# Forgetting-attention denominators in four 32-column groups, summed at the end of a query tile

## The chip, the cores and the metric

The kernel runs on the 8 cores of one Trainium2 chip. Each core works on one sequence of the batch and needs no other core. The metric is the device time of the slowest core in microseconds. Below, PE is TensorE, ACT is ScalarE, DVE is VectorE and POOL is GpSimd.

## The reference

One decoder layer on x of shape 8 x 2048 x 2048 (batch, sequence, model width). A combined projection feeds two groups of 8 heads each, with head size 128. What the change touches is the first group, forgetting attention (called FoX in the kernel):

```
s = q @ k.T * scale + cum[query] - cum[key]     # cum: running sum of log f
s = where(key <= query, s, -inf)
p = softmax(s)                                  # exp(s) / sum over the keys
o = p @ v
```

The kernel takes exp(s) without the division, sums it over the keys (the denominator), and multiplies the finished o by one over that sum. The second group is sliding-window attention with sinks. The output projection, norms, and a squared-ReLU MLP with d_ff 8192 follow.

## The kernel before

Everything is laid out with features on the partitions and tokens along the free dimension. The order of all work is written by one Python program. Each engine gets its own instructions in the order in which the program emits them, and waits are put in where one engine needs what another made. So an instruction that waits holds up all that were emitted behind it on its engine.

FoX runs head by head (8 heads), in `fox` (L1079), over query tiles j = 0 to 3 of 512 tokens, and inside a tile over 4j+4 key blocks kb of 128 keys. That is 40 steps in a head, 320 in all. In the last four blocks of a tile only the columns from c0 = 0, 128, 256, 384 on are computed, since the rest is masked. A step is made of three parts:

- `qk` (L1028): PE multiplies the key block by the query tile into one of three score banks (SF); in the last four blocks it adds the mask.
- `expo` (L1049): DVE subtracts the forget bias, in place in the bank; ACT writes exp of it as bf16 into one of NPB = 6 buffers Pb.
- `pv` (L1058): PE adds v times Pb into the output bank (OB[0], bank 4), and a 128x128 matrix of ones times Pb into the denominator bank (DB, bank 6). So every one of the 128 partitions of that bank holds the full sum over keys.

The loop at L1110 emits for step i: `qk` of step i+3 (LA = 3, L1075), filler, `pv` of step i, `expo` of step i+3, filler. A score bank is taken again three steps later, so `qk` of i+6 needs the exp of i+3 to be done.

The filler is other PE work that is fed in between (`Fill`, L700): projections of later heads in groups of 16 matmuls of 512 columns, evacuated by ACT or DVE from two banks, and the columns of the modulation (`mod_slot`, L485). `fw` (L1100) says how much is fed in. In heads 0 and 1 it is some 11 matmuls a step; in heads 2 to 6 it is 128 / 41.5, that is 3.08 a step, given half before `pv` and half after the step's `expo`. They come in bursts of four. In head 7 the filler is the first output tile, fed from its seventh step on.

`mod_slot` already uses the groups of 32 columns. Four matmuls with weights of 128x32 (`condpad`) write partitions 0-31, 32-63, 64-95 and 96-127 of one bank, each with its own moving operand of 512 columns. `fg_mm` (L768) does the same.

At the end of a query tile, `pv` emits the normalisation: ACT takes Ln of the denominators into `rr`, DVE copies the output bank to SBUF (`acc`), ACT takes Exp of -`rr`, DVE multiplies the two into `mix`. The next tile's first `pv` writes the same two banks, so it waits for the Ln and for the copy.

Of the kernel before, what the change touches and what calls it, by code (L numbers as in the profile page):

```python
# [7 lines left out]
BF16 = mybir.dt.bfloat16  # L8
AF = mybir.ActivationFunctionType
ALU = mybir.AluOpType  # L10
# [5 lines left out]
TS = 512  # L16
# [325 lines left out]
def program(nc, stack, orders, dry, T):  # L342
# [7 lines left out]
    B = T["bufs"]  # L350


    mix, mixF, hT = B["mix"], B["mixF"], B["hT"]
# [10 lines left out]
    rstd = [B["rstd0"], B["rstd1"]]  # L364
    rr, stage = B["rr"], B["stage"]
    qrot = B["qrot"]
    cosT, sinT = B["cosT"], B["sinT"]
    ident, maskc, mswa = B["ident"], B["maskc"], B["mswa"]
    Ctok, condpad, wfg = B["Ctok"], B["condpad"], B["wfg"]
# [3 lines left out]
    lf, Cf = B["lf"], B["Cf"]  # L373
    ones, modT, bmod, gv, Av = B["ones"], B["modT"], B["bmod"], B["gv"], B["Av"]
    onesF = B["onesF"]
    sqb = [B["sq0"], B["sq1"]]
    accs = [B["acc0"], B["acc1"]]
    WO = [B[f"WO{i}"] for i in range(16)]
# [10 lines left out]
    def mm(out, lhsT, rhs, start, stop):  # L389
        return (out.ap, lhsT.ap, rhs.ap, start, stop)  # L390

    def pe(mms, r, w, extra=()):
        def fn(e):
            ins = None
            for (o, l, rh, st, sp) in mms:
                ins = e.matmul(o, lhsT=l, rhs=rh, start=st, stop=sp)  # L396
            return ins
        return P.op("pe", fn, r, w, extra=extra)

    def act(out, in_, func, bias=None, scale=1.0):  # L400
        r = [in_]
        kw = {}
        if isinstance(bias, Acc):
            r.append(bias)
            kw["bias"] = bias.ap
        elif bias is not None:
            kw["bias"] = bias
        if isinstance(scale, Acc):
            r.append(scale)
            kw["scale"] = scale.ap  # L410
        else:
            kw["scale"] = scale
        return P.op("act", lambda e: e.activation(out=out.ap, in_=in_.ap, func=func, **kw), r, [out])  # L413

    def tt(out, a, b, op, eng="dve"):
        return P.op(eng, lambda e: e.tensor_tensor(out=out.ap, in0=a.ap, in1=b.ap, op=op), [a, b], [out])  # L416
# [12 lines left out]
    def cp(out, a):  # L429
        return P.op("dve", lambda e: e.tensor_copy(out=out.ap, in_=a.ap), [a], [out])  # L430
# [40 lines left out]
    class St:  # L471
        sb = 0
        pb = 0
        ob = 0
# [290 lines left out]
    F = Fill()  # L765
# [259 lines left out]
    def fox_list(h):  # L1025
        return [(h, j, kb) for j in range(NT) for kb in range(4 * j + 4)]

    def qk(st):  # L1028
        h, j, kb = st
        if kb == 0:  # L1030
            n = 4 * h + j
            for m in range(n, n + len(cfs)):
                if m // 4 < 8 and (m < 8 or h >= 2) and (m // 4, m % 4) not in cf_slot:
                    cf_load(m // 4, m % 4)
        bk = banks[SF[St.sb % 3]]
        St.sb += 1
        c0 = max(0, kb - 4 * j) * 128
        diag = kb >= 4 * j
        q = qT[h % 2](slice(j * TS + c0, j * TS + TS))
        kk = kT[h % 2](slice(kb * 128, kb * 128 + 128))  # L1040
        mms = [mm(bk(c0, TS), kk, q, True, not diag)]
        r = [kk, q]
        if diag:
            mms.append(mm(bk(c0, c0 + 128), ident(), maskc(), False, True))
            r += [ident(), maskc()]
        pe(mms, r, [bk()])
        steps[st] = (bk, c0)

    def expo(st):  # L1049
        h, j, kb = st  # L1050
        bk, c0 = steps[st]
        tt(bk(c0, TS), bk(c0, TS), cf_slot[(h, j)](slice(c0, TS)), ALU.subtract)
        p = Pb[St.pb % NPB]
        St.pb += 1
        act(p(slice(c0, TS)), bk(c0, TS), AF.Exp, bias=Ctok(slice(kb * 8 + h, kb * 8 + h + 1)))
        steps[st] = (p, c0)

    def pv(st):  # L1058
        h, j, kb = st
        p, c0 = steps.pop(st)  # L1060
        nkb = 4 * j + 4
        ob = banks[OB[0]]
        db = banks[DB]
        v = V_OF[h](kb, slice((h % 2) * 128, (h % 2) * 128 + 128))
        pp = p(slice(c0, TS))
        pe([mm(ob(c0, TS), v, pp, kb == 0, kb == nkb - 1), mm(db(c0, TS), ones(), pp, kb == 0, kb == nkb - 1)],
           [v, pp, ones()], [ob(), db()])
        if kb == nkb - 1:
            os = accs[1]
            act(rr(), db(), AF.Ln)  # L1070
            cp(os(), ob())
            act(rr(), rr(), AF.Exp, scale=-1.0)
            tt(mix(h, slice(j * TS, j * TS + TS)), os(), rr(), ALU.mult)

    LA = 3  # L1075

# [2 lines left out]
    def fox(segs, after=None):  # L1079

        L = [st for sg in segs for st in fox_list(sg[0])]
        n = len(L)
        seg = {sg[0]: sg for sg in segs}

        def begin(i):
            h, j, kb = L[i]
            if h in done:
                while done[h] < j:
                    F._one()
            qk(L[i])  # L1090

        jobs = {sg[0]: sg[1]() for sg in segs if sg[0] < 7}
        hs = [sg[0] for sg in segs]

        def push(h):
            F.main += jobs[h] if h in jobs else seg[h][1]()
            nx = hs[hs.index(h) + 1:]
            F.upnext = jobs[nx[0]][0] if nx and nx[0] in jobs else after

        def fw(i):  # L1100
            h = L[i][0]
            pos = i % 40
            return seg[h][2] / (40 - seg[h][3] + LA / 2) / 2 if pos >= seg[h][3] else 0

        push(hs[0])
        for i in range(LA):
            begin(i)
            F.fill(fw(i))
            expo(L[i])
        for i in range(n):  # L1110
            if i and i % 40 == 0:
                push(L[i][0])
            if i + LA < n:
                begin(i + LA)
            F.fill(fw(i))
            pv(L[i])
            if i + LA < n:
                expo(L[i + LA])
            F.fill(fw(i))


    SPB = Pb
# [87 lines left out]
    def qk_(h):  # L1210
# [7 lines left out]
        def gen():  # L1218
# [9 lines left out]
    j3 = qk_(3)  # L1228
    j6 = vpair(I_V + 6, vX)
    fox([(0, lambda: [sk_(0), svpair(), sq_(0), sq_(1), sq_(2), sq_(3)], 64 * 5 + 128, 0),  # L1230
         (1, lambda: [sk_(1), sq_(4), sq_(5), sq_(6), sq_(7), qk_(2)], 64 * 7, 0)], j3)
    F.drain()
# [107 lines left out]
    def last_head():  # L1340
# [8 lines left out]
    cfs.append(qrot)  # L1349
    St.cf = 0  # L1350
    fox([(2, lambda: [vpair(I_V + 4, vZ)], 128, 0)]
        + [(h, lambda h=h: [qk_(h + 1)], 128, 0) for h in range(3, 7)]
        + [(7, last_head, 4 * 34, 6)])
# [198 lines left out]
def build():  # L1552
# [33 lines left out]
    B = {}  # L1586

    def buf(name, off, dims, dt):
        B[name] = Buf(nc, name, off, dims, dt)
        return off + B[name].nbytes  # L1590
# [12 lines left out]
    o = RS  # L1603
    for i in range(5):
        o = buf(f"ring{i}", o, [2048], BF16)
    for nm in ("qT0", "kT0"):
        o = buf(nm, o, [S], BF16)
    buf("Cf", o, [S], F32)
    o = buf("vts", o, [16, 256], BF16)
    buf("lf", o, [S], F32)  # L1610
    buf("vZ", o, [16, 256], BF16)
    o = buf("skT", o, [2, S], BF16)
    for i in range(2):
        buf(f"rstd{i}", o, [TS], F32)
        o = buf(f"cfb{i}", o, [TS], F32)
# [4 lines left out]
    for nm in ("qT1", "kT1"):  # L1620
        o = buf(nm, o, [S], BF16)
    o = buf("vX", o, [16, 256], BF16)
# [3 lines left out]
    for i in range(NPB):  # L1626
        o = buf(f"Pb{i}", o, [TS], BF16)
    o = buf("stage", o, [TS], F32)
    o = buf("rr", o, [TS], F32)
    buf("wfg", o, [KC * 32], BF16)  # L1630
    o = buf("qrot", o, [TS], F32)
    o = buf("ident", o, [128], BF16)
    o = buf("maskc", o, [128], BF16)
    o = buf("mswa", o, [256], BF16)
    o = buf("Ctok", o, [128], F32)
    o = buf("condpad", o, [KC, 32], BF16)
# [7 lines left out]
    o = RS  # L1644
    for i in range(2):
        o = buf(f"Y{i}", o, [16, TS], F32)
    for i in range(NRB):
        o = buf(f"rung{i}", o, [2048], BF16)
# [7 lines left out]
    o = max(o, end1)  # L1656
    o = buf("ones", o, [128], BF16)
    o = buf("onesF", o, [128], F32)
    o = buf("bvb", o, [8], BF16)
    o += 112  # L1660
    o = buf("wob", o, [16], F32)
    o += 64
    o = buf("modT", o, [96], F32)
    o = buf("bmod", o, [96], F32)
    o = buf("gv", o, [4, KC], F32)
    o = buf("Av", o, [4, KC], F32)
    for i in range(2):
        buf(f"qh{i}", o + 4096 * i, [2048], BF16)
    for i in range(2):
        o = buf(f"sq{i}", o, [TS], F32)  # L1670
    for i in range(4):
        buf(f"sqs{i}", o - 4096 + 1024 * i, [256], F32)
    for i in range(2):
        o = buf(f"acc{i}", o, [TS], F32)
    assert BASE + o <= nc.sbuf_usable_end, (BASE + o, nc.sbuf_usable_end)
    T["bufs"] = B
    with ExitStack() as stack:
        T["banks"] = [Bank(stack.enter_context(nc.psum_tensor(f"bank{i}", [128, 512], F32)), i) for i in range(8)]
        orders = program(nc, stack, {}, True, T)
        program(nc, stack, orders, False, T)  # L1680
# [50 lines left out]
```

How the kernel before makes its waits and increments, by code:

```python
                def body(e, mine=mine):  # L259
                    have = {}
                    for o, ws in mine:
                        need = {}
                        for d in ws:
                            s, v = d.sig
                            need[s] = max(need.get(s, 0), v)
                        for s, v in need.items():
                            if have.get(s, 0) < v:
                                e.wait_ge(sems[s], v)
                                have[s] = v
                        if o.fn is not None:
                            ins = o.fn(e)
                            if o.sig is not None:
                                ins.then_inc(sems[o.sig[0]], 16 if o.dsem is not None else 1)
```

## Time and profile before

| what | value |
|---|---|
| median of 3 runs (range) | 2980.88 us (2980.04 to 3171.43) |
| the profiled execution | 2982.57 us, span of its slowest core (core 5) 2981.0 us |
| spans of the 8 cores | 2970.1 to 2981.0 us, granted clock 0.992 to 0.997 |
| PE busy | 2865.3 us, 96% of the span |
| DVE busy | 942.0 us, 32% |
| ACT busy | 776.5 us, 26% |
| POOL busy | 449.2 us, 15% |
| FoX, heads 0 and 1 | some 236 to 500 us from the span's start |
| sliding-window heads | some 500 to 617 us |
| FoX, heads 2 to 7 | some 617 to 978 us |

The profile is of the slowest core. Matmuls are pipelined: a row's duration reaches into the next matmul, so what a matmul costs is read as the distance from its start to the next start. An idle time in brackets on a row is what stood between the modelled end of the one before and this start, and names what ended it.

### The profile page before, as it was taken

To read this page: it belongs to the slowest core of one execution; us is meant where nothing else is said; L and a number is where in the kernel's file an instruction comes from. 1 tells how busy PE (TensorE), PEld (TensorE's weight loads), DVE (VectorE), ACT (ScalarE), POOL (GpSimd) and SP (SyncE) were. 2 spreads that over 40 slices of the span, in tenths; PEclk is the share of its full clock that TensorE was granted. 3 is DMA by queue.
4 is the path that set the end of the run, shared out by engine and by line. 5 is a ranking of instruction groups with operands and counts; after the bars stand their busy time and mean duration, and the time that the engine had idled before them with its cause. 6 is when DMAs were issued, how large, how long until landed. Compare 5 with 4: busy or idle time off the path is not lost.

```text
span 2981.0 us, 39533 instructions; the slowest of 8 cores (2970.1 to 2981.0 us)
## 1 busy us (share of the span) xinstructions
PE 2865.3 (96%) x15292; PEld 1393.3 (47%) x15292; DVE 942.0 (32%) x1510; ACT 776.5 (26%) x1276; POOL 449.2 (15%) x597
## 2 busy tenths in 40 slices
PE   3899999999998999999999999999999999999997
PEld 1466444664444444444444444444444444444446
DVE  1434664455554476431111000000333101111015
ACT  2213454655554355331111000000211000111112
POOL 1010000000001565300000111111000000000222
PEclk9999999999999999999999999999999999999999
DMA  9966665335544334644444555555788544445844
GB/s 218 213 117 119 104 106 93 64 65 92 89 82 92 99 129 169 127 78 77 75 75 78 92 98 95 91 99 109 160 188 190 95 74 75 78 78 109 155 76 149
DMA packets 107032, 325.96 MB, mean 109 GB/s; under 512 B 11584, under 2 KB 28224, under 8 KB 100448
## 3 DMA queue, kind: packets, MB, share of 16 engines
q0 software_dynamic: 58320, 211.97, 44.2%
q1 hardware_dynamic: 48528, 111.46, 11.5%
q8 instruction: 124, 2.03, 0.3%
q14 instruction: 60, 0.49, 0.1%
HBM read 493.32 MB, written 42.01 MB: 180 GB/s over the span
## 4 chain that ended last, share of the span: by engine, by line
PE 86%; DVE 3%; DMA 3%; ACT 3%; issue 2%; POOL 2%; DVEq 0%; ACTq 0%; POOLq 0%; SPq 0%
PE bank L396 86%; DMA rmod<-wMA 3%; POOL acc L416 2%; DVE bank L416 1%; ACT rr L413 1%; ACT Pb L413 1%; ACT sq L413 1%; DMA cfb<-crow 0%; ACT qrot L413 0%; DVE sq L421 0%; DVE bank L421 0%; DVE Y L416 0%; ACT acc L413 0%; DVE y L416 0%; DMA rung<-wD 0%
## 5 line engine op out<-in xcount | busy, mean ns | idle before, releaser
L396 PE MATMUL bank<-mix,rung 128*128 128x512 bf16 x4096 | 885.0, 379 | 0.0
L396 PE MATMUL bank<-a,rung 128*128 128x512 bf16 (+1 forms) x4096 | 858.4, 372 | 1.7 <-DMA rung<-wD 1.7
L396 PEld LDWEIGHTS bank<-mix,rung 128*128 128x128 bf16 x4096 | 400.8, 98 | 484.3 <-issue 1.7
L396 PEld LDWEIGHTS bank<-a,rung 128*128 128x128 bf16 x4096 | 400.7, 98 | 458.4 <-issue 1.9
L396 PE MATMUL bank<-hT,ring 128*128 128x512 bf16 x1536 | 397.0, 382 | 1.7 <-DVE sq L421 1.3
L413 ACT ACTIVATE a<-bank 128x512 bf16<-128x512 f32 x256 | 152.8, 597 | 914.4 <-DVE bank L427 913.5
L427 DVE TENSOR_SCALAR bank<-bank 128x512 f32<-128x512 f32 x256 | 166.1, 695 | 647.1 <-PE bank L396 647.1
L413 ACT ACTIVATE Pb<-bank,Ctok 128x512 bf16<-128x512 f32 (+1 forms) x320 | 193.0, 623 | 268.2 <-DVE bank L416 265.6
L396 PE MATMUL bank<-mix,WO 128*128 128x512 bf16 x1024 | 234.1, 382 | 13.5 <-ACT sq L413 12.2
L416 POOL TENSOR_TENSOR acc<-acc,sq 128x512 f32<-128x512 f32 x172 | 215.8, 1267 | 187.5 <-ACT sq L413 182.5
L396 PEld LDWEIGHTS bank<-hT,ring 128*128 128x128 bf16 x1536 | 146.4, 98 | 155.8 <-issue 10.3
L207 POOL DMA_DIRECT2D rung<-wU x128 | 68.1, 532 | 743.9 <-PE bank L396 710.0
L207 POOL DMA_DIRECT2D rung<-wD x124 | 66.2, 534 | 717.5 <-PE bank L396 689.2
L396 PE MATMUL bank<-ring,hT 128*128 128x256 bf16 x1280 | 169.5, 278 | 3.5 <-DVE bvb L430 2.6
L416 DVE TENSOR_TENSOR bank<-bank,cfb 128x512 f32<-128x512 f32 x240 | 142.3, 614 | 80.2 <-PE bank L396 74.3
L396 PEld LDWEIGHTS bank<-mix,WO 128*128 128x128 bf16 x1024 | 98.2, 98 | 136.3 <-issue 27.3
L430 DVE COPY mixF<-bank 128x512 f32<-128x512 f32 x32 | 20.6, 686 | 421.4 <-PE bank L396 421.4
L396 PEld LDWEIGHTS bank<-ring,hT 128*128 128x128 bf16 x1280 | 125.5, 100 | 47.4 <-issue 13.7
L396 PE MATMUL bank<-Pb,ones 128*128 128x512 bf16 (+3 forms) x444 | 130.8, 328 | 0.0
L413 ACT ACTIVATE sq<-bank 128x512 f32<-128x512 f32 x30 | 17.9, 597 | 396.5 <-DVE mixF L430 396.5
L396 PE MATMUL bank<-qT,kT 128*128 128x512 bf16 (+1 forms) x320 | 112.3, 352 | 9.1 <-ACT Pb L413 8.7
L207 POOL DMA_DIRECT2D ring<-wMB x64 | 33.8, 528 | 349.5 <-PE bank L396 337.8
(145 smaller groups left out, 1765.7 us busy)
## 6 DMA issues: line engine op xcount, KB each, us to landing
rung<-wU POOLq DMA_DIRECT2D x128, 512.0 KB, 6.3
rung<-wD POOLq DMA_DIRECT2D x124, 512.0 KB, 6.3
ring<-wMB POOLq DMA_DIRECT2D x64, 512.0 KB, 6.7
ring<-wA POOLq DMA_DIRECT2D x34, 512.0 KB, 6.4
Y<-xP SPq DMA_DIRECT2D x16, 1024.0 KB, 6.1
x1s<-Y SPq DMA_DIRECT2D x16, 1024.0 KB, 3.9
xstA<-xP SPq DMA_DIRECT2D x8, 1024.0 KB, 15.9
rmod<-wMA POOLq DMA_DIRECT2D x16, 512.0 KB, 21.8
```

Of the source, the lines that this page charges most:

```text
L207: return self.op(eng, lambda e: e.dma_start(out=oa, in_=ia), [in_], [out], dsem=dsem, extra=extra)
L396: ins = e.matmul(o, lhsT=l, rhs=rh, start=st, stop=sp)
L413: return P.op("act", lambda e: e.activation(out=out.ap, in_=in_.ap, func=func, **kw), r, [out])
L416: return P.op(eng, lambda e: e.tensor_tensor(out=out.ap, in0=a.ap, in1=b.ap, op=op), [a, b], [out])
L427: return P.op(eng, lambda e: e.tensor_scalar(out=out.ap, in0=a.ap, scalar1=sc, scalar2=None, op0=op), r, [out])
L430: return P.op("dve", lambda e: e.tensor_copy(out=out.ap, in_=a.ap), [a], [out])
```

## The change

The matmul of ones moves out of the step. Steps only collect their Pb buffer in `held`. At every fourth key block (kb % 4 == 3) the four collected blocks are summed together. In the query tiles j = 1 to 3 that is one group of four matmuls with weights of ones 128x32, each into its own 32 partitions of the denominator bank; the groups of a tile add up there. So each set of 32 partitions holds the sum over every fourth block. In tile j = 0 the four matmuls keep the full 128x128 ones.

At the end of a tile with j > 0, `den_split` writes the bank in two bf16 parts into `rrh`: ACT copies it (the high part), and DVE subtracts that copy from the bank (the low part). It is emitted behind the `expo` of that step. Two steps later, `den_fin` multiplies both parts by the 128x128 ones into the denominator bank. That adds up the 128 partitions, so the sum is 32 times too large, which the Ln's scale of 1/32 takes out. The Ln, the Exp and the multiplication into `mix` come after it, two steps later than before, in all tiles. The copy of the output bank stays where it was. `rrh` lies in the same bytes as `rr`. At the end of a call of `fox`, 12 units of filler are fed before the last `den_fin`.

```diff
+    rrh = B["rrh"]
+    ones32 = ones().re(ones.h[:, 0:32])
...
+    held = []
+    later = []
+
     def pv(st):
         h, j, kb = st
         p, c0 = steps.pop(st)
...
-        pe([mm(ob(c0, TS), v, pp, kb == 0, kb == nkb - 1), mm(db(c0, TS), ones(), pp, kb == 0, kb == nkb - 1)],
-           [v, pp, ones()], [ob(), db()])
+        pe([mm(ob(c0, TS), v, pp, kb == 0, kb == nkb - 1)], [v, pp], [ob()])
+        held.append((p, c0))
+        if kb % 4 == 3:
+            mms = []
+            for c, (pc, cc0) in enumerate(held):
+                if j:
+                    mms.append(mm(db(cc0, TS, p=(32 * c, 32 * c + 32)), ones32, pc(slice(cc0, TS)), kb == 3, kb == nkb - 1))
+                else:
+                    mms.append(mm(db(cc0, TS), ones(), pc(slice(cc0, TS)), c == 0, c == 3))
+            pe(mms, [pc(slice(cc0, TS)) for pc, cc0 in held] + [ones()], [db()])
+            del held[:]
         if kb == nkb - 1:
             os = accs[1]
-            act(rr(), db(), AF.Ln)
             cp(os(), ob())
-            act(rr(), rr(), AF.Exp, scale=-1.0)
-            tt(mix(h, slice(j * TS, j * TS + TS)), os(), rr(), ALU.mult)
+            return (h, j, db)
+        return None
+
+    def den_split(e):
+        h, j, db = e
+        if j:
+            act(rrh(0), db(), AF.Copy)
+            tt(rrh(1), db(), rrh(0), ALU.subtract)
+
+    def den_fin(e):
+        h, j, db = e
+        if j:
+            pe([mm(db(), ones(), rrh(i), i == 0, i == 1) for i in range(2)], [ones(), rrh()], [db()])
+        act(rr(), db(), AF.Ln, scale=1.0 / 32 if j else 1.0)
+        act(rr(), rr(), AF.Exp, scale=-1.0)
+        tt(mix(h, slice(j * TS, j * TS + TS)), accs[1](), rr(), ALU.mult)
...
             F.fill(fw(i))
-            pv(L[i])
+            e = pv(L[i])
             if i + LA < n:
                 expo(L[i + LA])
+            if e:
+                den_split(e)
+                later.append((i + 2, e))
             F.fill(fw(i))
+            if later and later[0][0] == i:
+                den_fin(later.pop(0)[1])
+        F.fill(12)
+        for _, e in later:
+            den_fin(e)
+        del later[:]
...
     o = buf("stage", o, [TS], F32)
+    buf("rrh", o, [2, TS], BF16)
     o = buf("rr", o, [TS], F32)
```

## Rows read from the trace of the kernel before

**Rows 1.** The page, the chain of work that ended last, by engine and by line.

```profile
PE 86%; DVE 3%; DMA 3%; ACT 3%; issue 2%; POOL 2%; DVEq 0%; ACTq 0%; POOLq 0%; SPq 0%
PE bank L396 86%; DMA rmod<-wMA 3%; POOL acc L416 2%; DVE bank L416 1%; ACT rr L413 1%; ACT Pb L413 1%; ACT sq L413 1%; DMA cfb<-crow 0%; ACT qrot L413 0%; DVE sq L421 0%; DVE bank L421 0%; DVE Y L416 0%; ACT acc L413 0%; DVE y L416 0%; DMA rung<-wD 0%
```

**Rows 2.** Stretches: us, then busy us (count) of PE, PEld, DVE, ACT, POOL.

```profile
236.00:500.00 264.00, 258.43 (x1606) 129.24 (x1604) 147.29 (x240) 111.99 (x197) 25.28 (x48) 1.00 0.60 101
...
617.00:978.00 361.00, 333.67 (x1985) 168.53 (x1983) 196.66 (x342) 186.24 (x313) 30.17 (x49) 0.98 0.49 87
```

**Rows 3.** Groups of instructions on TensorE; busy us, mean ns, idle before.

```profile
L396 PE MATMUL bank<-mix,rung 128*128 128x512 bf16 x4096 | 885.0, 379 | 0.0
...
L396 PE MATMUL bank<-ring,condpad 128*32 128x512 bf16 x256 | 25.6, 389 | 1.3 <-DVE modT L416 1.3
```

**Rows 4.** Order of time on TensorE; columns start us, us, instruction, count.

```profile
242.94 1.03 PE L396 MATMUL bank<-hT,ring 128*128 128x512 bf16 x4
243.90 0.40 PE L396 MATMUL bank<-ring,condpad 128*32 128x512 bf16 x4
244.23 1.04 PE L396 MATMUL bank<-hT,ring 128*128 128x512 bf16 x4
```

**Rows 5.** Order of time, all engines, around the end of a query tile (head 6).

```profile
863.61 0.38 PE L396 MATMUL bank<-qT,kT 128*128 128x512 bf16 x1
...
863.93 0.27 PE L396 MATMUL bank<-Pb,ones 128*128 128x256 bf16 x1
...
864.04 1.03 PE L396 MATMUL bank<-hT,ring 128*128 128x512 bf16 x4
864.09 0.70 DVE L416 TENSOR_TENSOR bank<-bank,cfb 128x512 f32<-128x512 f32 x1 [0.70 <-PE bank L396]
...
864.88 0.69 ACT L413 ACTIVATE Pb<-bank,Ctok 128x512 bf16<-128x512 f32 x1 [0.72 <-DVE bank L416]
...
865.12 0.22 PE L396 MATMUL bank<-Pb,vX 128*128 128x128 bf16 x1
...
865.45 1.03 PE L396 MATMUL bank<-hT,ring 128*128 128x512 bf16 x4
865.49 0.60 ACT L413 ACTIVATE rr<-bank 128x512 f32<-128x512 f32 x1
865.50 0.69 DVE L430 COPY acc<-bank 128x512 f32<-128x512 f32 x1 [0.71 <-PE bank L396]
866.18 0.63 ACT L413 ACTIVATE rr<-rr 128x512 f32<-128x512 f32 x1
...
866.45 0.38 PE L396 MATMUL bank<-Pb,vX 128*128 128x512 bf16 x1
...
866.91 0.69 DVE L416 TENSOR_TENSOR mix<-acc,rr 128x512 bf16<-128x512 f32 x1 [0.72 <-ACT rr L413]
...
867.52 1.89 DVE L416 TENSOR_TENSOR bank<-bank,cfb 128x512 f32<-128x512 f32 x3
...
868.31 1.88 ACT L413 ACTIVATE Pb<-bank,Ctok 128x512 bf16<-128x512 f32 x3 [1.50 <-DVE bank L416]
...
869.14 0.38 PE L396 MATMUL bank<-qT,kT 128*128 128x512 bf16 x1 [0.59 <-ACT Pb L413]
...
872.80 0.38 PE L396 MATMUL bank<-qT,kT 128*128 128x512 bf16 x1
```

**Rows 6.** The same view, TensorE, a tile end with more beside it (head 5).

```profile
824.76 0.22 PE L396 MATMUL bank<-Pb,vZ 128*128 128x128 bf16 x1
...
834.74 0.38 PE L396 MATMUL bank<-qT,kT 128*128 128x512 bf16 x1
```

**Rows 7.** Who waited for whom, 617 to 980 us; total us, times, longest.

```profile
PE bank L396 <- ACT Pb L413: 8.7, 15, 1.6
...
PE bank L396 <- ACT rr L413: 4.2, 6, 1.2
PE bank L396 <- DVE acc L430: 3.0, 4, 0.9
```

## Prediction

> **What bounds the kernel now.** I read the chain of waits first: 86% of it is TensorE's matmuls [rows 1]. So time is won by giving PE less to do, or lost by making it wait. Next, the busy times of the two stretches with FoX [rows 2]. In heads 0 and 1 PE is busy 258.4 of 264 us for 80 steps, 3.3 us a step. In heads 2 to 7 it is busy 333.7 of 361 us for 240 steps, 1.5 us a step; DVE and ACT are busy only 54% and 52% there, yet PE has gaps. Then the waits [rows 7]: PE waited 8.7 us for an exp (it had to free a score bank), 4.2 us for ACT's `rr` and 3.0 us for the copy of the output bank, all at tile ends. Last, one tile end in order of time [rows 5], to see which chain makes these gaps.
>
> A gap is wider than its bracket, since the bracket starts at a matmul's modelled end. A full matmul costs 885.0 / 4096 = 0.216 us from start to start [rows 3], while its row lasts 0.38.
>
> **What leaves PE.** The cost of a ones matmul goes with its columns: 256 columns took 0.11 us (863.93 to 864.04) [rows 5]. Each of the 24 tiles with j > 0 has four masked-end blocks of 512, 384, 256 and 128 columns, together 2.5 full ones: 24 x 2.5 x 0.216 = 13.0 us. Before these stand 4, 8 or 12 full blocks, 24 in a head, 192 in all: 41.5 us. Together 54.5 us go. The eight j = 0 tiles keep theirs.
>
> **What comes to PE.** 48 full groups and 24 masked-end ones, 72 groups of four. The kernel before has this very operation in its modulation columns. The burst at 242.94 should hand over after 4 x 0.216 at 243.80; the four start at 243.90, and the next matmul at 244.23 [rows 4]. So the group costs 0.43 us, twice one matmul and half of four. 48 such places in the trace lie between 0.42 and 0.44, this one stands for them. The whole of the 256 gives the same order: 25.6 us of busy time for 64 groups is 0.40 [rows 3]. 72 x 0.43 = 31.0 us. The bounds are 0.22 (one matmul) and 0.86 (four in a row); I take 0.43, the same shape measured. In a masked-end group the longest member still has 512 columns, so I take no less there. The final sums add 24 x 2 x 0.216 = 10.4 us. PE's work: -54.5 + 31.0 + 10.4 = **-13.1 us**.
>
> The Trainium skill has a rule that prices the group otherwise (TensorE: Matmul & The Clock Gate, Measured speedup vs the span model): a packed group spans one matmul plus about 4 ns for each further tile. By it, a group would be an estimated 0.23 us and PE's work 14 us less again. The same skill's TensorEngine Tiling (Array Packing), Key Properties, says that changing the tiling mode drains the array; the 0.1 us that stands ahead of the group at 243.90 agrees with the second page, so the sum goes by the row.
>
> **What the moved end of a tile costs.** Two things come to the in-order queues: ACT's copy and DVE's subtraction (24 each, some 0.6 and 0.7 us by the nearest rows, the Ln and the copy of the output bank). In busy time both engines have room. What counts is the order. Call the start of the tile's last `pv` zero (865.12) and take the links from [rows 5]: `pv` to copy of the output bank 0.38; DVE to its next instruction 0.61 (866.91 to 867.52); DVE to the ACT instruction that needs it 0.79 (867.52 to 868.31); ACT to its next 0.60 (three in 1.88, the last taking 0.69); ACT to ACT that needs it 0.69 (Ln to Exp); ACT to DVE 0.73 (866.18 to 866.91); ACT to a PE that waits 0.83 (868.31 to 869.14); DVE to a waiting PE 0.95 (865.50 to 866.45).
>
> Before: Ln 0.37, Exp 1.06, product 1.79, bias of step i+3 at 2.40, exp 3.19, PE's `qk` of i+6 at 4.02. All read straight off the rows. PE's work up to there is 0.11 + 2 x 0.216 + 4 x 0.216 + two bursts of filler 1.73 = 3.13, so 0.89 us is lost, of which the row's bracket shows 0.59 and the rest is the copy's wait at 866.45 and the modelled tail.
>
> After: copy of the output bank 0.38, bias of i+3 at 0.99, exp 1.78, ACT's copy 2.38, subtraction 3.11, bias of i+4 at 3.72 and of i+5 at 4.33, exp of i+5 5.12. The final sum on PE can start at 3.11 + 0.95 = 4.06. PE gets there after `pv` and group 0.49, two `qk` and two `pv` 0.86, and 2.5 steps of filler 1.66, at 3.0: it stops for a microsecond, and behind it stands all its work, since PE is in order. The Ln stands on ACT behind the exp of i+5: 5.72, Exp 6.41, product 7.14, and behind it on DVE the bias of i+6 at 7.75, exp 8.54, and `qk` of i+9 on PE at **9.37**. PE's work from zero to there is 0.49 + ten `qk` and `pv` 2.16 + final sum 0.43 + the next group 0.43 + 5.5 steps of filler 3.65, or four bursts 3.45 as in these rows: 6.96. So 2.4 us are lost, in two places (final sum, `qk` of i+9) and a little at the next group, which waits for the Ln at 5.72 + 0.83.
>
> Before, the same stretch runs from 865.12 to 872.80, 7.68 us. So a clean end grows by 1.7, of which 0.16 is more work inside it (0.43 x 3 against 1.13 us of ones); the lost time grows by 1.5. Four of the ten j = 1 and 2 ends in heads 2 to 6 take 7.68 or 7.69. The longest takes 9.98 (824.76 to 834.74) [rows 6]: evacuations of filler stand in its queues, and PE has a modulation group besides. I add the same lateness to the chain but the room grows too, and there I take no growth. Over all I take 0.9 us, between 0 and 1.5, weighted by four clean ends in ten. 17 ends in heads 2 to 7 have j > 0 and a next tile; those that lead into a new head have shorter blocks in chain and work alike. 17 x 0.9 = **+15.3 us**.
>
> **What costs nothing.** The six such ends in heads 0 and 1: PE has 5.5 steps x 3.3 = 18 us of work over a chain of 9.4; without that filler they would cost the same 1.5. The j = 0 ends: no split, and the Ln moves behind the exp of i+5, so the chain ends at about 7.6 against some 6.9 of work, a loss as large as now. `expo` of i+3 must wait at every group for the release of its Pb buffer, but its bias and link (0.48 from `qk`, 863.61 to 864.09, and 0.79) take as long as PE needs from that `qk` through filler, `pv` and group (1.3 us); it is due three steps later. The last end is covered by 12 matmuls of filler (2.6 us). No DMA is added or moved.
>
> Sum: -13.1 + 15.3 = +2.2 us on the profiled execution's 2982.57, which lies 1.7 above the median of the runs. That gives 2984.8 for such an execution, 2983 as a median; I say **2984**.
>
> **The rivals.**
>
> *Slower: the wait for ACT's copy on DVE.* Behind the blocked subtraction also lie filler evacuations, and one ahead of the chain adds its 0.6 to 0.7. If every end pays 1.5 + 0.6, it is 17 x 2.1 = 35.7 - 13.1 = +22.6: 3005. For it speaks that each engine is in order and every link above is measured. Against it: the ends with evacuations already have longer PE work. It decides from 13.1 / 17 = 0.8 us an end; above that the kernel gets slower. Chance 0.24.
>
> *Faster: the ends get no worse.* The old chain to `qk` of i+6 is gone (it would be ready at 1.78 + 0.83 = 2.6), and if PE has enough beside the new one, only the -13.1 is left, or with half of today's loss (17 x 0.9 / 2) -21: 2962 to 2970. Against it stand 9.37 us of chain over 7 us of work. Chance 0.21.
>
> *The groups do not run side by side.* Then 72 x 0.86 + 10.4 - 54.5 = +17.8, and with the ends 3016. Weights of ones from one tile, four Pb buffers as moving operands: nothing in that differs from [rows 4]. Chance 0.03.
>
> *The groups cost one matmul.* If the 0.2 us around the modulation groups belongs to their own weights or neighbours, a group costs 0.22 to 0.23, PE's work falls 14 us more, and what of it lies inside the chains is lost again, about half: 2970 to 2977. This is what the span model of the Trainium skill's clock gate page would bring. 48 places without an exception speak against it. Chance 0.05.
>
> **How the numbers follow.** The forecast has 0.47, its own range 2975 to 2993. The range that leaves out two in ten reaches from the faster rival to the slower one, 2960 to 3006. What a measurement can tell from no change is 2%, 60 us; no case reaches that far. Slower by more needs groups in a row and ends of 3 us together, 0.02; faster by more has no mechanism, 0.01; within 2%: 0.97.
>
> **What would show it.** Groups of four `ones` of 128x32, 0.43 from start to start; a PE wait for DVE's `rrh` of about 0.9 us, 17 times in heads 2 to 7; DVE waiting for ACT's `rrh`, 0.7 or more each; PE's wait for an exp coming 9 us after a tile's end, not 4; heads 0 and 1 shorter by some 3 us (a quarter of 13.1), heads 2 to 7 longer by some 5. Wrong it would be if heads 2 to 7 got shorter, or if heads 0 and 1 did not.

## Result and the profile after

The changed kernel took 2999.82 us (median of 5 runs, 2995.56 to 3293.65) against 2980.88 us (5 runs): ratio 1.0064, 95% interval [1.0051, 1.0077]. It is slower by 19 us, inside the predicted range of 2960 to 3006, 16 us above the predicted 2984.

Times of single executions below are those of the profiled ones, and ratios leave out executions in which cores ran at a lowered clock throughout.

Rows that name no core are those of a kernel's slowest core: 5 in the kernel before, 4 in the changed one, 3 in e6.

First the page of the changed kernel: span, busy time of PE, DVE and ACT, and the chain by engine.

```profile
span 2998.0 us, 39742 instructions; the slowest of 8 cores (2990.3 to 2998.0 us)
...
PE 2859.8 (95%) x15340; PEld 1376.1 (46%) x15340; DVE 952.1 (32%) x1534; ACT 787.3 (26%) x1300; POOL 450.2 (15%) x597
...
PE 85%; DVE 4%; ACT 3%; DMA 3%; issue 3%; POOL 2%; DVEq 0%; ACTq 0%; POOLq 0%
```

PE's busy time fell from 2865.3 to 2859.8 us while the span grew by 17 (of two profiled executions; the 19 us are of medians): PE has less to do and waits more. Its new instructions in heads 2 to 7, in groups as in [rows 3]:

```profile
L398 PE MATMUL bank<-Pb,ones 128*32 128x512 bf16 x162 | 21.8, 400 | 2.4 <-ACT rr L415 2.4
...
L398 PE MATMUL bank<-rrh,ones 128*128 128x512 bf16 x36 | 10.7, 377 | 7.2 <-DVE rrh L418 7.0
```

And who waited for whom there (total us, times, longest), the answer to [rows 7]:

```profile
ACT Pb L415 <- PE bank L398: 29.8, 22, 3.7
...
PE bank L398 <- ACT sq L415: 14.2, 6, 4.7
PE bank L398 <- ACT Pb L415: 11.2, 15, 1.1
...
PE bank L398 <- DVE rrh L418: 7.0, 12, 1.0
PE bank L398 <- DVE acc L432: 6.6, 9, 1.8
...
PE bank L398 <- ACT acc L415: 4.4, 1, 4.4
```

PE's waits for an exp are 11.2 us (8.7 before), there are 7.0 us of waits for the split's low part, 6.6 for the copy of the output bank (3.0), and, in head 7 and just behind it, 14.2 and 4.4 for the output tile's squares and first sum (7.7 and 1.3 before, shown further below). The first row is the release of held buffers: ACT waited 29.8 us for PE, but ACT is not the bound.

Where the 19 us are, from PE's first `qk` of head 0, of head 2 and of head 7, its last `pv`, and its first matmul of the MLP:

| stage, us | before, core 1 | before, core 5 | after, core 1 | after, core 5 |
|---|---|---|---|---|
| heads 0, 1 and the sliding-window heads | 389.8 | 390.2 | 387.4 | 385.2 |
| heads 2 to 6 | 280.5 | 282.1 | 289.0 | 288.6 |
| head 7 | 72.3 | 77.1 | 84.6 | 84.5 |
| to the MLP | 210.8 | 210.8 | 214.5 | 214.5 |

So packing pays where filler is plentiful (2 to 5 us), heads 2 to 6 lose 6 to 9, head 7 loses 7 to 12, and the stage behind it 4. Past that point, cores 1 and 5 take as long as before to about 1 us.

The clean tile end of the changed kernel in order of time (head 6, the tile of [rows 5]):

```profile
863.37 0.22 PE L398 MATMUL bank<-Pb,vX 128*128 128x128 bf16 x1
...
863.52 0.39 PE L398 MATMUL bank<-Pb,ones 128*32 128x512 bf16 x4
863.70 0.69 DVE L432 COPY acc<-bank 128x512 f32<-128x512 f32 x1 [0.54 <-PE bank L398]
...
863.85 0.39 PE L398 MATMUL bank<-qT,kT 128*128 128x512 bf16 x1
...
865.09 0.69 ACT L415 ACTIVATE Pb<-bank,Ctok 128x512 bf16<-128x512 f32 x1 [1.15 <-PE bank L398]
...
865.68 0.59 ACT L415 ACTIVATE rrh<-bank 128x512 bf16<-128x512 f32 x1
866.37 0.69 DVE L418 TENSOR_TENSOR rrh<-bank,rrh 128x512 bf16<-128x512 f32 x1 [1.37 <-ACT rrh L415]
866.98 1.29 DVE L418 TENSOR_TENSOR bank<-bank,cfb 128x512 f32<-128x512 f32 x2
...
867.21 0.59 PE L398 MATMUL bank<-rrh,ones 128*128 128x512 bf16 x2 [0.60 <-DVE rrh L418]
...
867.76 1.28 ACT L415 ACTIVATE Pb<-bank,Ctok 128x512 bf16<-128x512 f32 x2 [1.50 <-DVE bank L418]
...
868.94 0.59 ACT L415 ACTIVATE rr<-bank 128x512 f32<-128x512 f32 x1
...
869.62 0.63 ACT L415 ACTIVATE rr<-rr 128x512 f32<-128x512 f32 x1
...
869.68 0.40 PE L398 MATMUL bank<-Pb,ones 128*32 128x512 bf16 x4 [0.15 <-ACT rr L415]
...
870.36 0.69 DVE L418 TENSOR_TENSOR mix<-acc,rr 128x512 bf16<-128x512 f32 x1 [1.51 <-ACT rr L415]
...
870.97 1.89 DVE L418 TENSOR_TENSOR bank<-bank,cfb 128x512 f32<-128x512 f32 x3
...
871.75 1.88 ACT L415 ACTIVATE Pb<-bank,Ctok 128x512 bf16<-128x512 f32 x3 [1.50 <-DVE bank L418]
...
872.58 0.38 PE L398 MATMUL bank<-qT,kT 128*128 128x512 bf16 x1 [1.11 <-ACT Pb L415]
```

Every link of the predicted chain that these rows show is there. From the last `pv` at 863.37: ACT's copy 2.31 later (predicted 2.38), subtraction 3.00 (3.11), final sum 3.84 with a wait of 0.60 (4.06), Ln 5.57 (5.72), product 6.99 (7.14), bias of i+6 7.60 (7.75), and `qk` of i+9 at 9.21 after a wait of 1.11 (9.37). The group costs 0.43 beside FoX's own work: `pv` of 128 columns at 863.37 takes 0.06, and the next `qk` starts at 863.85. The wait for the split's low part was forecast as some 0.9 us, 17 times; it came 12 times, 7.0 us together.

### The profile page after: what moved, and what is told of

Same layout as the page of the kernel before. It is cut to its first block, busy times and chain, and to the rows that moved or that the text cites. A ratio compares the mean times of both kernels' runs of the same rounds, so it can differ in the third digit from the quotient of the medians.

```text
span 2998.0 us, 39742 instructions; the slowest of 8 cores (2990.3 to 2998.0 us)
## 1 busy us (share of the span) xinstructions
PE 2859.8 (95%) x15340; PEld 1376.1 (46%) x15340; DVE 952.1 (32%) x1534; ACT 787.3 (26%) x1300; POOL 450.2 (15%) x597
## 4 chain that ended last, share of the span: by engine, by line
PE 85%; DVE 4%; ACT 3%; DMA 3%; issue 3%; POOL 2%; DVEq 0%; ACTq 0%; POOLq 0%
PE bank L398 85%; DMA rmod<-wMA 3%; POOL acc L418 2%; DVE bank L418 1%; ACT Pb L415 1%; ACT rr L415 1%; ACT sq L415 1%; DVE acc L432 0%; DVE bank L423 0%; ACT qrot L415 0%; DVE Y L418 0%; DVE sq L423 0%; ACT rrh L415 0%; DMA rung<-wD 0%; ACT acc L415 0%
## 5 line engine op out<-in xcount | busy, mean ns | idle before, releaser
L398 PE MATMUL bank<-qT,kT 128*128 128x512 bf16 (+1 forms) x320 | 113.0, 354 | 11.7 <-ACT Pb L415 11.2
L432 DVE COPY y<-bank 128x512 f32<-128x512 f32 x32 | 20.6, 686 | 191.7 <-PE bank L398 191.7
```

## The experiments

Each was a full kernel on all 8 cores. Stages as above, heads 2 to 6 / head 7 / to the MLP, on one core with all matmul records (core 1, but 2 for e1 and 5 for e4); before is 280.5 / 72.3 / 210.8 and the change 289.0 / 84.6 / 214.5. The cores of one execution differ, in heads 2 to 6 and in the last stage by up to 3 us and in head 7 by up to 5. Differences in the text are between profiled executions (before 2982.57). The ratios carry the spread of all executions that they take in, so the intervals are wide beside the differences here.

| kernel | profiled execution, us | ratio to before [95%] | stages, us |
|---|---|---|---|
| the change | 2999.82 | 1.0064 [1.0051, 1.0077] | 289.0 / 84.6 / 214.5 |
| e1 packed, old end | 2969.00 | 0.9943 [0.9912, 0.9975] | 274.1 / 74.0 / 211.1 |
| e2 held, full ones, late end | 3000.26 | 1.0021 [0.9979, 1.0064] | 276.7 / 83.5 / 211.2 |
| e3 packed, late end, no final sum | 2964.75 | 0.9936 [0.9913, 0.9959] | 269.2 / 82.2 / 211.1 |
| e4 split early | 2989.84 | 1.0012 [0.9986, 1.0037] | 276.9 / 83.5 / 217.1 |
| e5 product late | 2974.01 | 0.9972 [0.9949, 0.9995] | 272.6 / 78.7 / 217.0 |
| e6 both | 2962.55 | 0.9915 [0.9879, 0.9950] | 263.6 / 78.4 / 216.0 |
| e7 both, head 7 alone | 2994.57 | 1.0034 [1.0002, 1.0067] | 288.6 / 79.2 / 215.7 |
| e8 both, and the last product later | 2958.26 | 0.9949 [0.9918, 0.9981] | 263.2 / 77.5 / 212.6 |
| e9 as e8, output tile 0 evacuated at once | 2942.09 | 0.9875 [0.9854, 0.9896] | 263.1 / 65.0 / 210.5 |
| e10 before, evacuated at once | 2967.43 | 0.9977 [0.9941, 1.0013] | 280.5 / 64.3 / 210.0 |
| e11 the change, evacuated at once | 2979.16 | 0.9994 [0.9952, 1.0036] | 290.1 / 68.6 / 211.0 |

**e1, packing alone.**

```diff
             os = accs[1]
+            act(rr(), db(), AF.Ln, bias=1.0)
             cp(os(), ob())
-            return (h, j, db)
+            act(rr(), rr(), AF.Exp, scale=-1.0)
+            tt(mix(h, slice(j * TS, j * TS + TS)), os(), rr(), ALU.mult)
```

> Groups of four as in the change, but the tile's end as before: Ln, Exp and product at the last pv, straight from the bank. The final sum over the groups is left out (each 32 partitions keep the sum of every fourth block, and the Ln takes a bias of 1). My theory (the packing saves PE what the rows say, the deferred end costs it): 54.5 - 31.0 = 23.5 us less PE work, and the tile ends lose 0.3 us more than before at 17 places, since the group stands ahead of the Ln: -18 us, ratio 0.994. Rival A (a group costs more than 0.43 us beside FoX's own work, up to four matmuls in a row): +7 to +12 us, ratio 1.002 to 1.004, and groups 0.86 apart in the trace. Rival B (holding the Pb buffers makes the exp wait): ratio near 1.00 with PE waiting for exps inside the tiles.

It came out at 2969.00, 13.6 us below before, where -18 was expected. Packing saves, and Rival A is out. Heads 2 to 6 gain 6.4 us, and in them PE's waits for exps grew from 6.1 to 17.8 us: the end's chain starts behind the group, and a shorter PE meets the same chain. All 17 of these waits stand at `qk` of step i+6 behind a tile's end and none inside a tile, so Rival B is out too.

**e2, holding and the late end alone.**

```diff
-                if j:
-                    mms.append(mm(db(cc0, TS, p=(32 * c, 32 * c + 32)), ones32, ...
-                else:
-                    mms.append(mm(db(cc0, TS), ones(), pc(slice(cc0, TS)), c == 0, c == 3))
+                mms.append(mm(db(cc0, TS), ones(), pc(slice(cc0, TS)), kb == 3 and c == 0, kb == nkb - 1 and c == 3))
...
     def den_split(e):
         h, j, db = e
-        if j:
-            act(rrh(0), db(), AF.Copy)
-            tt(rrh(1), db(), rrh(0), ALU.subtract)
+        return
...
     def den_fin(e):
         h, j, db = e
-        if j:
-            pe([mm(db(), ones(), rrh(i), i == 0, i == 1) for i in range(2)], ...
-        act(rr(), db(), AF.Ln, scale=1.0 / 32 if j else 1.0)
+        act(rr(), db(), AF.Ln, scale=1.0)
```

> Blocks held in fours and the end of the tile two steps late as in the change, but with 128x128 ones in all tiles, so no packing, no split, no final sum. PE's work is that of before. My theory: the chain without copy and subtraction ends at 7.55 us after the last pv against 7.3 us of PE work, so 0.3 us is lost at an end where 0.9 was: -10 us in heads 2 to 7, ratio 0.997. Rival B (holding the buffers, or the late Ln by itself, is what costs): as slow as the change, ratio 1.005 or more.

Half a miss. Heads 2 to 6 gain 3.8 us (10 were expected with head 7), so holding is not what costs. But head 7 went from 72.3 to 83.5: the late end, without copy, subtraction or final sum, makes nearly all of the change's loss there. Holding is in e2 as well, but also in e1, where head 7 takes 74.0 to 76.1. The ratio's interval holds 1, so the sum of both decides nothing; the stages do. (Its profiled execution reached FoX some 20 us late on two cores, so its 3000 says little.)

**e3, the change without split and final sum** (`den_split` returns at once, `den_fin` has no matmuls, the Ln takes bias=1.0 and scale=1.0).

> The change without ACT's copy, DVE's subtraction and PE's final sum (left out: the sum over the groups, and the Ln takes a bias of 1); Ln, Exp and product stay two steps late. My theory: 23.5 us less PE work, 0.7 us lost at an end instead of 0.9: -27 us against before, ratio 0.991, and against the change -46, of which 10.4 is the final sum's own work and the rest the chain. Rival A (dear groups): -27 + 31 = +4 us, ratio 1.001. Rival C (the late product alone makes the wait, the split has no part in it): ratio 1.003, since only the final sum's 10.4 us goes.

35 us below the change; -46 was expected. The sum over the groups is left out, as in e1. Heads 2 to 6 carry 20 of them, of which 30 final matmuls x 0.216 = 6.5 are work and 13 waiting: Rival C, by which only the final sum's own work would go, is out. Head 7 stays at 82.2 (79.3 to 83.1 on the cores), which is the larger part of what is missing. In e2 and e3, late end but no final sum, the stage behind head 7 takes 211.1 to 211.3 us: the 3.7 us that the change loses there come with the split and the final sum.

**e4, copy and subtraction ahead of the bias subtraction.**

```diff
             e = pv(L[i])
-            if i + LA < n:
-                expo(L[i + LA])
             if e:
                 den_split(e)
                 later.append((i + 2, e))
+            if i + LA < n:
+                expo(L[i + LA])
```

> The change with copy and subtraction emitted ahead of the expo of that step, not behind it. My theory: subtraction at 1.33 us after the last pv instead of 3.11, so the final sum can start at 2.3 while PE gets there at 3.0, no wait for rrh in the trace; exp of i+5 at 3.95, product 5.97, qk of i+9 at 8.2 instead of 9.2 to 9.4; an end loses 1.1 us instead of 2.4: 17 x 1.3 = 22 us less than the change, 2978, ratio to before 0.999. Rival C (only the late product counts): qk of i+9 waits as long as in the change, 2990 or more, ratio 1.003.

No wait for `rrh` is left, and the clean end takes 8.18 us (8.2 expected). Heads 2 to 6 are 12 us shorter than in the change; in all it is 10 us by the profiled executions, 12 by the medians, and not 22: head 7 and the stage behind it keep their losses.

**e5, the product one step later.**

```diff
         act(rr(), rr(), AF.Exp, scale=-1.0)
+
+    def den_mul(e):
+        h, j, db = e
         tt(mix(h, slice(j * TS, j * TS + TS)), accs[1](), rr(), ALU.mult)
...
+            if later and later[0][0] == i - 1:
+                den_mul(later.pop(0)[1])
             if later and later[0][0] == i:
-                den_fin(later.pop(0)[1])
+                den_fin(later[0][1])
         F.fill(12)
         for _, e in later:
             den_fin(e)
+            den_mul(e)
```

> The change with the product into mix emitted one step later, behind the expo of i+6, so that no bias subtraction stands behind it on DVE. Copy and subtraction stay behind the expo. My theory: the wait for the final sum stays (about 0.6 in the bracket), the wait of qk of i+9 goes: an end loses 1.2 us instead of 2.4, 20 us less than the change: 2980, ratio 1.000. Rival C' (the split alone is to blame): no change against it, ratio 1.006.

26 us below the change (20 expected): 16 in heads 2 to 6, 6 in head 7. PE still waits 6.9 us for the subtraction, and its waits for exps fell from 11.2 to 1.2.

**e6, both moves.**

> Both moves: copy and subtraction ahead of the expo, product one step later. My theory: neither wait is left, an end loses 0 to 0.2 us, and the packing's 13.1 us shows beside the loss of before that goes too (some 18 us): 2950, ratio 0.990. Rival A (groups dearer than 0.43): 2970 or more, ratio 0.997. Rival D (DVE and ACT are simply too full at a tile's end, whatever the order): at least half of today's waits stay, ratio 1.000 or more.

2962.55, 37 us below the change and 20 below before. The same tile end as above, in this kernel:

```profile
841.48 0.22 PE L398 MATMUL bank<-Pb,vX 128*128 128x128 bf16 x1
...
842.14 0.60 ACT L415 ACTIVATE rrh<-bank 128x512 bf16<-128x512 f32 x1
...
842.84 0.69 DVE L418 TENSOR_TENSOR rrh<-bank,rrh 128x512 bf16<-128x512 f32 x1 [0.34 <-ACT rrh L415]
...
843.44 1.89 DVE L418 TENSOR_TENSOR bank<-bank,cfb 128x512 f32<-128x512 f32 x3
...
844.55 0.59 PE L398 MATMUL bank<-rrh,ones 128*128 128x512 bf16 x2
...
846.01 0.59 ACT L415 ACTIVATE rr<-bank 128x512 f32<-128x512 f32 x1
...
847.42 0.69 DVE L418 TENSOR_TENSOR mix<-acc,rr 128x512 bf16<-128x512 f32 x1 [0.90 <-ACT rr L415]
...
848.51 0.38 PE L398 MATMUL bank<-qT,kT 128*128 128x512 bf16 x1
```

The subtraction comes 1.36 after the last `pv` instead of 3.00, the final sum at 844.55 waits for nothing, and `qk` of i+9 follows after 7.03 us. That is PE's own work as the prediction counted it, 6.96. Rival D (engines too full) is out: with the same instructions in another order, PE's waits in heads 2 to 6 for exps, the split, the copy and `rr` are 5.0 us together, against 24.7 in the change and 12.6 before. 2950 was expected; head 7 and the last stage, 6 and 5 us longer than before, hold most of the 12 us that lack.

**e7, both moves in head 7 alone.**

```diff
+    LATE = 7
...
             e = pv(L[i])
+            if e and e[0] == LATE:
+                den_split(e)
             if i + LA < n:
                 expo(L[i + LA])
+            if e and e[0] != LATE:
+                den_split(e)
             if e:
-                den_split(e)
                 later.append((i + 2, e))
...
```

(The lines left out emit the product one step later where `e[0] == LATE`.)

> Both moves, but in head 7 alone; heads 0 to 6 run as in the change. The trace of the change shows head 7 with 19 us of PE waits for ACT's acc and sq (the output tile's banks) where before had 9. My theory: these banks are freed late because the product blocks DVE ahead of their evacuation; with the product out of the way head 7 is as long as before or shorter (77 us to the last pv instead of 84.5) and the first output tile's wait of 3.6 us is again 1: 10 to 13 us less than the change, ratio 1.002. Rival E (they are a matter of the clock, which falls to its lower level in head 7): head 7 stays at 84, ratio 1.006.

5 us below the change, half of what was expected: head 7 fell from 84.6 to 79.2 (77.7 to 79.3 on the cores), not to 77 or less, and the last stage moved by no more than the cores differ. PE's waits for the output tile's first sum and squares in head 7 fell from 4.4 and 9.6 to 2.4 and 8.0 us, where before had 1.3 and 6.7. So the order at the ends is a part of head 7's loss, not all. The granted clock there, 0.89, is hardly above the change's 0.88.

**e8, both moves, and the last product later** (against e6).

```diff
         for _, e in later:
             den_fin(e)
+            F.fill(16)
             den_mul(e)
```

> Early split and late product in all heads (as in the fastest version so far, 2962 us), and at the end of each call of fox 16 more units of filler between the last Exp and the last product. The trace of the changed kernel has PE waiting 3.62 us after the last pv for ACT's square, where DVE took 3.13 us to wait for the Exp and then the product ahead of the output tile's evacuation; the kernel before and the version without the final sum wait 1.0 there. My theory: without the product in front, the evacuation runs 3.6 us earlier on DVE, and ACT's square stands only behind the Exp: PE's wait falls from 3.6 to about 2, 1.6 us less in all, ratio 0.993 to 0.9925. Rival: the wait comes from PE's own final sum, which stands behind 12 matmuls: then 3.6 stays.

This is the wait that it was meant for, in the changed kernel, just behind the last `pv`:

```profile
987.90 0.59 PE L398 MATMUL bank<-rrh,ones 128*128 128x512 bf16 x2
...
990.01 0.69 DVE L418 TENSOR_TENSOR mix<-acc,rr 128x512 bf16<-128x512 f32 x1 [3.13 <-ACT rr L415]
990.62 0.74 DVE L429 TENSOR_SCALAR Y<-bank,wob 128x512 f32<-128x512 f32 x1
...
991.46 0.69 ACT L415 ACTIVATE sq<-bank,wob 128x512 f32<-128x512 f32 x1 [1.55 <-DVE Y L429]
...
992.29 2.29 PE L398 MATMUL bank<-mix,WO 128*128 128x512 bf16 x5 [3.62 <-ACT sq L415]
```

DVE waits for the Exp and takes the product; the evacuation of an output bank (`Y`) and its square on ACT come after, and PE waits 3.62 us for the bank. In e8 the wait is 1.96 us (2 expected), and the stage went from 216.0 to 212.6 us. By the profiled executions e8 is 4 us faster than e6; by the ratios it is not, and the intervals of the two overlap, so the gain rests on the stage and the wait.

**e9, output tile 0 evacuated at once; e10 and e11, the same in before and in the change.**

```diff
-            if m:
+            if t == 0:
+                evac(m, bk)
+            elif m:
                 evac(m - 1, prev)
             prev = bk
-        evac(KC - 1, prev)
+        if t:
+            evac(KC - 1, prev)
```

> As e8_last_end, and output tile 0 (head 7's filler) evacuates each bank right behind its own 16 matmuls, not behind the next 16. My theory: PE's waits for ACT's sq in head 7 (8 to 10 us in all versions with the late end, 6.7 before) come from banks whose evacuation is emitted late and then stands behind the tile-end chain. With a whole group of matmuls in between they go, and with them the drops of the granted clock: head 7 from 78 us to about 68, 2950. Rival (DVE and ACT are too full in head 7): the waits move to FoX's exps, no gain.

> The kernel before with the same evacuation at once in output tile 0, so that it can be told from the rest. Theory: its 9 us of waits for acc and sq go, head 7 from 72 to 77 us to about 65 to 68: -8 us, ratio 0.997. Rival: as in e9, ratio 1.000.

> The change with that evacuation at once in output tile 0. Theory (half of the change's loss is head 7's output banks standing behind the blocked DVE): head 7 loses its 14 us of waits for acc and sq and the clock's drops: from 84.5 to about 70, so -14 us against the change, and only about +5 against e10's; ratio to before 1.002. Rival E (head 7's loss is FoX's own waits at 1.2 GHz): 84 stays within 3 us, ratio 1.006.

Head 7 fell to 65.0, 64.3 and 68.6 us (68, 65 to 68, and 70 were expected). The waits for the output banks are gone in all three. e10 gained 15 us (8 expected), e11 stands 21 below the change (14 expected) and still 12 above e10; the ratios of both have 1 in their intervals, so what is sure of them is the stages. In e11, heads 2 to 6, which this edit does not touch, are 7 to 10 us longer than in e10, head 7 is 4 to 7 longer, and the stretch before them 4 to 5 shorter. What the change added to head 7, 12.3 us on core 1, is with the banks out of the way 4.3 on core 1 (e11 against e10) and up to 7 on others, where e11 takes 71.3 and e10 64.3 to 65.9. Rival E, by which head 7 would have stayed at 84, is out. Busy times and granted clock (the first value behind the busy times of the five engines) of core 1 in head 7, before, the change, and e10:

```profile
895.00:975.00 80.00, 67.53 (x415) 32.99 (x414) 38.18 (x71) 36.74 (x60) 14.34 (x16) 1.00 0.48 109
```

```profile
902.00:986.00 84.00, 66.40 (x369) 28.65 (x368) 36.87 (x68) 35.92 (x59) 9.69 (x10) 0.88 0.38 81
```

```profile
896.00:960.00 64.00, 59.78 (x370) 29.12 (x368) 35.59 (x65) 33.88 (x57) 9.72 (x10) 1.00 0.49 108
```

The mean granted clock there is 1.00 before, 0.88 in the change and 1.00 in e10. So the change's head 7 has stretches at 1.2 GHz beside its longer waits. What the clock alone can do, the kernel before shows: on its cores 1 and 5 PE's waits in head 7 are the same 11.3 us, and the head takes 72.3 us at a granted clock of 1.00 and 77.1 at 0.93.

e9 is the fastest version: 2942.09 us, ratio 0.9875 [0.9854, 0.9896] (of two executions, 2942.09 and 2942.41), 40 us below before. Of these some 15 are the evacuation (16 from e8 to e9, 15 from before to e10), which has nothing to do with the change.

## Why the prediction was right, and what it missed

The direction, the mechanism and the sizes of the clean case held. The sum was -13.1 + 15.3 = +2.2; +19 was measured. That this lies in the range is in part luck: the range reaches up to 3005 for the slower rival, by which every end would lose 2.1 us. Nothing of the kind happened in heads 2 to 6. There the forecast comes to +5.3 (15 x 0.9 less five eighths of 13.1), and +6.5 to +8.5 was measured. For head 7 and the stage behind it, it comes to +0.2, and +11 to +16 was measured. So heads 2 to 7, forecast some 5 us longer, were 14 to 21 longer.

- *PE's work, -13.1.* Held. 62 of the groups in the changed kernel's core 5 could be measured between neighbours without a wait: median 0.424 us, against 0.43 taken from the modulation columns. Both rivals about the group (four in a row, or one matmul's time) are out: the groups are at 0.42, and e1 is faster than before. The group starts 0.09 us after its `pv` hands over (863.37 + 0.06 to 863.52); with that the drain at a change of tiling mode agrees (the Trainium skill, TensorEngine Tiling (Array Packing), Key Properties). The prediction's estimate of 0.23 misread the span model (the Trainium skill, TensorE: Matmul & The Clock Gate, Measured speedup vs the span model). The model gives a group's span from first start to last end, one matmul's duration plus about 4 ns for each further tile. With the row's duration of 0.38 us for one matmul that is an estimated 0.39, and the row of the group at 863.52 agrees with 0.39. So the rival by which the groups cost one matmul's 0.216 was not the model's either. What the group costs beside its neighbours, 0.42, is another thing: the four start within 0.01 us, cost one matmul's 0.216 together, and have about 0.1 us ahead of them and as much behind.
- *The chain at an end, +1.5 in the clean case.* Held to some 0.2 us at each link (the final sum is the farthest, 3.84 against 4.06). e4 and e5 take one wait away each, e6 both.
- *The mean of 0.9 an end.* The stretch from last `pv` to `qk` of i+9 was to grow by 0.9 + 0.16. In heads 2 to 6 it grew by 1.3 (j = 1: 8.16 to 9.48, mean of five), 1.0 (j = 2: 8.95 to 9.92) and 1.6 (j = 3: 7.82 to 9.46). The stretches of j = 3 reach past the j = 0 end of the next head, so they cannot be added up. Cut at each tile's last `pv`, a head grew by 1.5 us, with an estimated 1.6 us less work in it: 3.1 us more were lost in a head, for which the forecast had 3 x 0.9 = 2.7. As a mean 0.9 was near; it had been chosen between 0 and 1.5, not worked out.
- *"The j = 0 ends: a loss as large as now".* This failed. Their stretches grew by 0.95 us too (8.00 to 8.95). The chain of the tile before has not ended when the four steps of a j = 0 tile are over, and both use DVE in order, and `accs[1]`. Head 5's j = 0 end in the changed kernel:

```profile
794.06 0.22 PE L398 MATMUL bank<-Pb,vZ 128*128 128x128 bf16 x1
...
794.64 0.69 DVE L418 TENSOR_TENSOR mix<-acc,rr 128x512 bf16<-128x512 f32 x1 [1.50 <-ACT rr L415]
...
795.25 0.69 DVE L418 TENSOR_TENSOR bank<-bank,cfb 128x512 f32<-128x512 f32 x1
795.86 0.68 DVE L432 COPY acc<-bank 128x512 f32<-128x512 f32 x1
...
796.68 0.38 PE L398 MATMUL bank<-Pb,vZ 128*128 128x512 bf16 x1 [0.77 <-DVE acc L432]
```

  The last `pv` is at 794.06. The copy of its bank could start 0.33 later, but DVE has the late product of head 4's last tile first, then a bias, and copies at 795.86; PE waits 0.77 us at the next `pv`. Between the last `pv` of j = 3 and that of j = 0 PE lost no more than before, so what the two ends cost comes together behind the j = 0 end. All four ends of a head, with its 3.1 us, make the 1 to 3 us by which heads 2 to 6 came out above the forecast.
- *Head 7.* This is the step that failed most: it was counted as two more ends at 0.9, and the last end as covered by its 12 matmuls. Measured +7 to +12, and +3.7 behind it. The filler of head 7 is an output tile whose banks need DVE and then ACT, emitted only behind the next bank's matmuls. The changed kernel there (head 7, j = 1):

```profile
927.50 0.34 PE L398 MATMUL bank<-bvb,WO 128*128 128x1 bf16 x8
...
929.27 0.63 ACT L415 ACTIVATE rr<-rr 128x512 f32<-128x512 f32 x1
930.00 0.69 DVE L418 TENSOR_TENSOR mix<-acc,rr 128x512 bf16<-128x512 f32 x1 [2.09 <-ACT rr L415]
930.61 0.74 DVE L429 TENSOR_SCALAR Y<-bank,wob 128x512 f32<-128x512 f32 x1
931.45 0.69 ACT L415 ACTIVATE acc<-bank,wob 128x512 f32<-128x512 f32 x1 [1.55 <-DVE Y L429]
...
932.28 1.01 PE L398 MATMUL bank<-mix,WO 128*128 128x512 bf16 x2 [4.44 <-ACT acc L415]
```

  The evacuation to `Y` stands behind the product, which waits for the Exp, which stands behind the exp of i+5. PE, in order, stops 4.44 us at the output matmul. Before, it stopped 1.3 us there; this is who it waited for in head 7 and just behind it (core 1):

```profile
PE bank L396 <- ACT sq L413: 7.7, 6, 2.0
...
PE bank L396 <- ACT acc L413: 1.3, 1, 1.3
```

  What the prediction said of the clean tile ("behind it stands all its work") holds for the filler's own evacuations. It had named them as lying behind the blocked subtraction, but priced only the one ahead of the chain. That the last end's PE part is covered was right (the final sum at 987.90 waits for nothing); its product was not.
- *Heads 0 and 1.* Forecast some 3 us shorter: 3.1 us on core 1 and 5.9 on core 5 up to their last `pv` (2.4 to 5 with the sliding-window heads).
- *The held buffers.* Counted at nothing, and PE pays next to nothing for it: in e6, where most other waits are gone, PE waits 0.6 us for exps in heads 2 to 6, with the buffers held as in the change.

Left open: how the loss in head 7 splits between waiting and clock, since the kernel with its waits and no lowered clock was not made. PE's waits there grew from 11.3 to 17.4 us and its work fell by an estimated 1.6, so on core 1 some 8 of the 12.3 us are neither, and on core 5, whose clock was lowered before as well, some 3 of 7.4. How far the clock makes these is not shown.

## What to carry to other kernels

When a step is moved later on in-order queues, follow not only its own chain but everything that comes to stand behind it on each engine, up to the first buffer that the bound engine takes again; here the same instructions were worth +17 us or, in another order, -20 (profiled executions). Where a matmul's partial result is finished by two engines in turn, emit the instruction that depends on the other engine behind the next work that does not. And a stretch that is fed with other filler than the rest (head 7) needs its own reading; a mean over clean tiles doesn't price it.

## What was unexpected of the hardware

The granted clock in head 7 of the change, core 1, in two stretches (busy times of the five engines, then the clock):

```profile
908.00:918.00 10.00, 7.08 (x37) 2.95 (x36) 5.29 (x9) 5.91 (x10) 0.86 (x2) 0.76 1.01 218
918.00:928.00 10.00, 10.00 (x59) 4.43 (x58) 4.63 (x10) 3.59 (x8) 0.00 (x0) 0.90 0.94 162
```

PE was busy 7.08 of 10 us in the first, with waits for `rr` and the output bank's copy of 1.0 and 1.8 us, and the granted clock fell to 0.76 over that stretch, that is, part of it ran at 1.2 GHz. Behind these waits the four output matmuls that begin at 915.88 start 0.43 us apart instead of 0.216. In e10, where the long waits are gone, the mean over head 7 is 1.00 on core 1 and 0.97 on core 3, in e11 0.98 and 0.93. So waits this short, in an engine that was 71% busy, went with a lowered clock. The Trainium skill (TensorE: Matmul & The Clock Gate, Part 1) says that an array left idle is put back to half rate; the rows agree on the half rate, and what preceded it here was no long idle time.
